# Two of seven weight rests made by a transfer that adds, in a two-block transformer kernel

## The chip, the cores and the metric

One core of one Trainium2 chip runs the whole kernel. The time is device time in microseconds of that core for one execution. Five engines have instruction streams of their own, and meet through semaphores: TensorE (PE; its weight loads are listed as PEld), VectorE (DVE), ScalarE (ACT), GpSimd (POOL) and SyncE (SP, here only a queue of transfers).

## The reference

The kernel computes a stack of transformer blocks on 512 tokens with a model width of 1024: a block with gated delta-rule attention and one with stick-breaking attention, each followed by a SwiGLU feed-forward layer, and then a third block with latent and windowed attention and a convolutional feed-forward layer. The change touches only the two SwiGLU layers:

```python
def swiglu(x, w_gu, w_down):
    g, u = jnp.split(x @ w_gu, 2, axis=-1)
    return (jax.nn.silu(g) * u) @ w_down

h = h + swiglu(rms_norm(h, ffn_norm[layer]), ffn_w_gu[layer], ffn_w_down[layer])
```

The gate and up matrices together are 1024 x 5632 and the down matrix 2816 x 1024, all float32. The result must hold to float32 accuracy.

## The kernel before, in words

**Products in three passes.** TensorE multiplies rounded float32 (the type fp32r). Every operand is therefore split into a rounded part (`wh`, `xh`) and its rest (`wl`, `xl`), and a product is three matmuls: rounded by rounded, rounded weight by rest of the input, rest of the weight by rounded input (`three`, lines 2331 to 2333). ScalarE makes the rounded part of a weight tile by a copy into fp32r, and VectorE the rest by a subtraction.

**The stream of weights.** All weights lie in one tensor, `stream`, as units of 128 x 2048 float32, 1 MB each. SP loads unit u into `raw[:, u % 2]` (`load`) once the unit that was there is used up: it waits for the semaphores `hi_made` and `lo_made`, which count units whose last quarter has been rounded and whose last rest is made.

**Seven products in place of eight.** The two SwiGLU layers ("ffn0" and "ffn1", function `ffn_fast` on each engine) hold most of their work as 24 units with a scheme of seven products of half size in place of eight (the Strassen-Winograd form). Tokens are halved (256 each), and a unit's four quarters of 128 x 512 are the four blocks of the weight matrix. Products 0, 1, 3, 5 and 6 read a quarter of `raw`, two of which VectorE has overwritten with sums by then; products 2 and 4 read the sums in `wsum`. A product is called a piece here: (j, k) is piece k of unit j. Of each unit, pieces 1 and 6 use quarters 1 and 3 as they came from memory. A piece is four blocks of three matmuls with 256 columns. The 24 units are 16 gate units (a gate tile and its up tile) and two groups of 4 down units.

**The order.** `ORDER` lists the 168 pieces of a layer: (0, 0), and then for each unit j the pieces 2, 1, 4, 3 of j, piece 0 of j + 1, and 5 and 6 of j. So piece (j, 6) stands at position 7j + 7. Each engine walks this list at its own step p, with fixed leads: at step p ScalarE copies out the result of the piece at p - 1 (pieces 0, 2, 4), does the silu if the piece at p - 2 was a 5, and rounds the weights of piece p + 5 (`HI_LEAD`); VectorE makes the rest of piece p + 4 (`LEAD`), the sums for piece p + 6 (`SUM_LEAD`), and joins or adds the result of piece p - 1; after a whole gate unit it multiplies gate and up (`gated`). In some units it also prepares a pair of hidden tiles as operands of the down products (`pair_sums`, `pair_lo`, lines 1397 to 1410; ScalarE does `pair_hi`). All of it is in order on each engine, so a wait holds everything behind it.

**Places of the pieces.** The rounded parts and rests have eight slots of 128 x 512 each; a slot is free when TensorE has done the piece eight positions before.

**The lines.** 657 is ScalarE's rounding of a piece (`hi`), 1483 VectorE's rest of a piece (`lo`), 1454 and 1456 the first two sums, 1461 and 1467 the other two, 617 the silu, 674 the copy out, 1498, 1504 and 1509 the joins of pieces 1, 3 and 5, 1520 the addition of a down piece, 1379 and 1380 the product of gate and up, 1366 the wide product of the six plain gate units that go before the stretch, 493 the load of the stream, 2253 GpSimd's eight transfers of 256 KB at another place of the kernel.

```python
def lo(j, k):
    half, w = weights_of(f, j, k)
    ...
    dve.tensor_tensor(wl[:, half, w], source_of(f, j, k), wh[:, half, w].bitcast(F32), ALU.subtract).then_inc(lo_made if k == 6 else part_lo, 1)
```

GpSimd does nothing in these stretches: it has a sum of squares before and one after.

Of the kernel before, what the change touches and what calls it, by code (L numbers as in the profile page):

```python
# [113 lines left out]
LEAD = 4  # L114
HI_LEAD = 5
SUM_LEAD = 6
SETS = ((4, 5, 0), (1, 2, 3))
BANK_OF = {0: 0, 2: 0, 3: 0, 6: 0, 1: 1, 4: 2, 5: 2}
QUARTER_OF = {0: (0, 0), 1: (0, 0), 2: (0, 1), 5: (0, 1), 4: (1, 1), 3: (1, 1), 6: (1, 0)}
# [39 lines left out]
SPLITS = running(lambda j, k: k != 6)  # L159
# [4 lines left out]
PAIR_SUMS_AT.update({DONE_AT[GATE_AT[2 * m + 1]] + 3: m for m in (3, 5, 6, 7)})  # L164
HIDDEN_AT = {DONE_AT[DOWN_AT[7]] + 1: REST, DONE_AT[DOWN_AT[7]] + 2: REST + 1}
HIDDEN_AT.update({DONE_AT[GATE_AT[n]] + 3: n for n in range(REST + 2, FC)})


def gu_count(f, n):
# [48 lines left out]
def build(nc, io):  # L218
    with ExitStack() as ctx:
# [137 lines left out]
        def mat(name):  # L357
# [60 lines left out]
        each = {part_hi: SPLITS[last_piece] + 3, part_lo: SPLITS[last_piece] + 3, prod_done: SPLITS[last_piece],  # L418
                weights_summed: 4 * len(STREAM), forked: FORKS[last_piece], joined: JOINS[last_piece], normed: 8,
                tokens_summed: 16, operand_hi: 12, operand_lo: 12, half_added: ADDS[last_piece], pair_summed: 4 * (REST // 2)}  # L420

        def fast_count(s, f, n):
            return before[s] + each[s] * f + n
# [15 lines left out]
        def piece_done(f, j, k):  # L439
            if k == 6:  # L440
                return units_used, stream_unit(FAST[f], j) + 1
            return prod_done, fast_count(prod_done, f, SPLITS[j, k])

        def slot_free(f, j, k):
            i = ORDER.index((j, k))
# [70 lines left out]
        def _(act):  # L516
# [92 lines left out]
            def ffn_fast(f, to, gain):  # L609
# [39 lines left out]
                def hi(j, k):  # L649
                    u = stream_unit(name, j)  # L650
                    half, w = weights_of(f, j, k)
                    if k in (2, 3, 4, 5):
                        act.wait_ge(weights_summed, fast_count(weights_summed, f, 4 * j + {4: 1, 2: 2, 3: 3, 5: 4}[k]))
                    else:
                        act.wait_ge(raw_landed[u % 2], 16 * (u // 2) + 16)
                    act.wait_ge(*slot_free(f, j, k))
                    act.activation(wh[:, half, w], source_of(f, j, k), ACT.Copy).then_inc(hi_made if k == 6 else part_hi, 1)  # L657

                def down_hi(q):
                    u = stream_unit(name, len(STREAM))  # L660
# [3 lines left out]
                    act.activation(wh[:, u % 2, w], raw[:, u % 2, w], ACT.Copy).then_inc(part_hi if q < 3 else hi_made, 1)  # L664

                def copy_out(j, k):
                    act.wait_ge(prod_done, fast_count(prod_done, f, SPLITS[j, k]))
                    last = gate_before(j)
                    if last is not None:
                        act.wait_ge(*join_made(f, last, {0: 1, 2: 5, 4: 3}[k]))  # L670
                    elif k == 4:
                        act.wait_ge(prod_made, FC * f + PLAIN)
                    to = scaled[:, 1, 0:TOK] if k == 4 else fork[:, k // 2, :]
                    act.activation(to, result_of(j, k), ACT.Copy).then_inc(forked, 1)

                def products():
                    for p in range(len(ORDER) + 4):
                        j, k = ORDER[p - 1] if 0 < p <= len(ORDER) else (None, None)
                        if j in GATES and k in (0, 2, 4):
                            copy_out(j, k)  # L680
                        j, k = ORDER[p - 2] if 1 < p <= len(ORDER) + 1 else (None, None)
                        if j in GATES and k == 5:
                            act.wait_ge(*join_made(f, j, 5))
                            silu(STREAM[j][1])
                        if p + HI_LEAD < len(ORDER):
                            hi(*ORDER[p + HI_LEAD])
                        elif p + HI_LEAD < len(ORDER) + 4:
# [11 lines left out]
                    token_sums(n)  # L699
                pair_hi(0)  # L700
                gate_up(4)
                for p in ORDER[:LEAD]:
                    hi(*p)
                gate_up(5)
                hi(*ORDER[LEAD])
                products()
                for i in range(3):
                    split_hi(u0 + 31 + i)
# [511 lines left out]
        def _(dve):  # L1220
# [50 lines left out]
            def split_out(name, to, gain):  # L1271

                u0, r = U0[name], RESID[name]
                for c in range(KC):
                    if c in (4, 6):
                        split_lo(u0 + 3 + (4, 6).index(c))
                    if c == KC - 1:
                        for x in range(KC - 1):
                            dve.wait_ge(resid_added, 8 * r + x + 1)
                            low_of_scaled(to, gain, x)  # L1280
                    if name == "mix_out":
                        dve.wait_ge(h_back[c], 16)
# [74 lines left out]
            def ffn_fast(f, to, to_gain):  # L1357
# [88 lines left out]
                def first_sums(j):  # L1446
                    u, q = stream_unit(name, j), raw_quarters(j)
                    dve.wait_ge(raw_landed[u % 2], 16 * (u // 2) + 16)
                    if j:
                        dve.wait_ge(part_lo, fast_count(part_lo, f, SPLITS[j - 1, 4]))  # L1450
# [12 lines left out]
                def last_sum(j):  # L1463
                    q = raw_quarters(j)
                    dve.wait_ge(weights_summed, fast_count(weights_summed, f, 4 * j + 2))
                    dve.wait_ge(part_lo, fast_count(part_lo, f, SPLITS[j, 1]))
                    dve.tensor_tensor(q[1], q[1], wsum[:, 1, :], ALU.subtract).then_inc(weights_summed, 1)

                def sums(j, k):
# [6 lines left out]

                def lo(j, k):
                    half, w = weights_of(f, j, k)
                    if k == 6:
                        dve.wait_ge(hi_made, stream_unit(name, j) + 1)  # L1480
                    else:
                        dve.wait_ge(part_hi, fast_count(part_hi, f, SPLITS[j, k]))
                    dve.tensor_tensor(wl[:, half, w], source_of(f, j, k), wh[:, half, w].bitcast(F32), ALU.subtract).then_inc(lo_made if k == 6 else part_lo, 1)  # L1483

                def down_lo(q):
                    u = stream_unit(name, len(STREAM))
                    w = slice(SEQ * q, SEQ * q + SEQ)
                    if q < 3:
                        dve.wait_ge(part_hi, fast_count(part_hi, f, SPLITS[last_piece] + q + 1))
# [31 lines left out]

                def products():
                    for p in range(len(ORDER) + 5):
                        if p + LEAD < len(ORDER):
                            lo(*ORDER[p + LEAD])
                        elif p < len(ORDER):
# [32 lines left out]
                pair_lo(0)  # L1559
                gate_up(4)  # L1560
                sums(*ORDER[1])
                for p in ORDER[:LEAD]:
                    lo(*p)
                sums(*ORDER[LEAD])
                gate_up(5)
                products()
# [595 lines left out]
        def _(pool):  # L2162
# [165 lines left out]
        def _(pe):  # L2328
# [115 lines left out]
            def ffn_fast(f):  # L2444
# [23 lines left out]
                def piece(j, k):  # L2468
                    kind, n = STREAM[j]
                    half, w = weights_of(f, j, k)  # L2470
                    if k == 6:
# [24 lines left out]
                def down_rest():  # L2496
                    u1, width = stream_unit(name, len(STREAM)), FC - REST
                    for i in range(3):
                        if i:
                            unit_ready(u1 + i)  # L2500
                        for b in (*range(5), *range(6, 11), 5, *range(11, BLOCKS)) if i == 0 else range(BLOCKS * i, BLOCKS * i + BLOCKS):
                            c, fc = b // width, b % width
                            if b in (0, 4, 8):
                                pe.wait_ge(part_hi, fast_count(part_hi, f, SPLITS[last_piece] + b // 4 + 1))
                                pe.wait_ge(part_lo, fast_count(part_lo, f, SPLITS[last_piece] + b // 4 + 1))
# [853 lines left out]
```

## Time and profile before

| | |
|---|---|
| Median of three runs | 2214.07 us (2213.58 to 2215.66) |
| The profiled execution | 2213.68 us, span 2211.8 us |
| Granted TensorE clock over the span | 0.997 |
| TensorE matmuls busy | 2147.3 us, 97% of the span |
| VectorE busy | 1460.8 us, 66% |
| ScalarE busy | 1082.7 us, 49% |
| GpSimd busy | 320.9 us, 15% |
| Transfers | 185.00 MB, mean 84 GB/s |

The busy time of an engine is the time in which it runs at least one instruction. TensorE's matmuls overlap and their ends are modelled, so the starts of successive matmuls say more than their lengths. A row of the timeline has the start from the beginning of the span, the duration, the engine, the line, the operation, its output and inputs with their shapes, and in brackets the idle time of the engine just before it, with the instruction that ended it.

### The profile page before, as it was taken

The page shows a single profiled execution, that of the slowest core. Times are in us where ns is not written, and L with a number is a line of the kernel's source. Part 1 is how long each engine was busy: PE and PEld are TensorE (multiplying, and loading weights), DVE is VectorE, ACT ScalarE, POOL GpSimd, SP SyncE. Part 2 cuts the span into 40 slices and gives each one's busy share as a digit, 9 for nine tenths or more (in the row PEclk, how much of TensorE's full clock was granted, in tenths as well). Part 3 has the DMA queues.
Part 4 walks back from the last instruction along what each step waited for, and adds up shares of the span by engine and source line. Part 5 has one row for each costly group of instructions (what it writes and reads, how often), then busy time and mean ns, then how long its engine had stood idle before and what let it go on. Part 6 is the DMA issues. An engine that isn't in the chain of part 4 may idle for free.

```text
span 2211.8 us, 33448 instructions
## 1 busy us (share of the span) xinstructions
PE 2147.3 (97%) x12698; PEld 1836.8 (83%) x12698; DVE 1460.8 (66%) x2344; ACT 1082.7 (49%) x1700; POOL 320.9 (15%) x267
## 2 busy tenths in 40 slices
PE   9999999998999999999999999999999999999998
PEld 6788887788999978877889989878778778888887
DVE  6766666479999843455689999556666665555522
ACT  5445555345454544565444555355565554444312
POOL 0221222310000030002200000300111144222211
PEclk9999999999999999999999999999999999999999
DMA  3311111221222322201213222331221222222221
GB/s 140 115 58 39 58 39 39 74 91 65 96 96 96 125 92 89 79 36 39 96 65 107 96 96 100 130 132 58 72 72 39 72 97 96 98 101 102 96 95 57
DMA packets 31675, 185.00 MB, mean 84 GB/s; under 512 B 3104, under 2 KB 7712, under 8 KB 11312
## 3 DMA queue, kind: packets, MB, share of 16 engines
q1 hardware_dynamic: 29520, 175.48, 22.9%
q0 software_dynamic: 2016, 7.60, 1.0%
q8 instruction: 95, 1.56, 0.3%
q14 instruction: 44, 0.36, 0.0%
HBM read 178.84 MB, written 7.37 MB: 84 GB/s over the span
## 4 chain that ended last, share of the span: by engine, by line
PE 74%; DVE 13%; ACT 5%; issue 4%; DMA 2%; SPq 0%; DVEq 0%; POOL 0%; ACTq 0%; POOLq 0%
PE ps L2331 20%; PE ps L2333 19%; PE ps L2332 19%; DVE wl L1483 3%; DMA raw<-in_stream 2%; PE ps L2657 2%; PE ps L3148 1%; ACT wh L525 1%; PE ps L3091 1%; PE ps L3131 1%; PE ps L2651 1%; DVE wsum L1454 1%; ACT wh L657 1%; PE ps L3158 1%; PE ps L2923 1%
## 5 line engine op out<-in xcount | busy, mean ns | idle before, releaser
L2331 PE MATMUL ps<-xh,wh 128*128 128x512 f32 (+1 forms) x1616 | 610.3, 378 | 13.3 <-DVE act_up L1380 9.4
L2333 PE MATMUL ps<-xh,wl 128*128 128x512 f32 (+1 forms) x1616 | 584.0, 361 | 0.0
L2332 PE MATMUL ps<-xl,wh 128*128 128x512 f32 (+1 forms) x1616 | 582.8, 361 | 0.0
L2331 PEld LDWEIGHTS ps<-xh,wh 128*128 128x128 f32 x1616 | 306.0, 189 | 63.4 <-issue 12.1
L2333 PEld LDWEIGHTS ps<-xh,wl 128*128 128x128 f32 x1616 | 305.1, 189 | 48.0
L2332 PEld LDWEIGHTS ps<-xl,wh 128*128 128x128 f32 x1616 | 306.0, 189 | 42.4 <-issue 4.3
L1229 DVE TENSOR_TENSOR wl<-raw,wh 128x2048 fp32r<-128x2048 f32 x92 | 212.8, 2313 | 175.7 <-ACT wh L525 175.6
L525 ACT ACTIVATE wh<-raw 128x2048 fp32r<-128x2048 f32 x92 | 175.9, 1912 | 161.1 <-PE ps L2333 160.8
L2331 PE MATMUL ps<-part_h,wh 128*128 128x256 f32 (+1 forms) x672 | 221.7, 330 | 6.0 <-DVE hT L1520 3.9
L2333 PE MATMUL ps<-part_h,wl 128*128 128x256 f32 (+1 forms) x672 | 220.3, 328 | 0.0
L2332 PE MATMUL ps<-part_l,wh 128*128 128x256 f32 (+1 forms) x672 | 219.8, 327 | 0.0
L657 ACT ACTIVATE wh<-raw 128x512 fp32r<-128x512 f32 x240 | 146.2, 624 | 96.6 <-DMA raw<-in_stream 57.6
L1483 DVE TENSOR_TENSOR wl<-raw,wh 128x512 fp32r<-128x512 f32 x240 | 165.1, 688 | 36.8 <-ACT wh L657 36.6
L2331 PE MATMUL ps<-t_h,wh 128*128 128x256 f32 x512 | 146.4, 286 | 17.7 <-DVE scaled L1504 10.7
L2331 PEld LDWEIGHTS ps<-part_h,wh 128*128 128x128 f32 x672 | 126.2, 188 | 22.0 <-issue 5.9
L2333 PE MATMUL ps<-t_h,wl 128*128 128x256 f32 x512 | 143.7, 281 | 0.0
L2332 PE MATMUL ps<-t_l,wh 128*128 128x256 f32 x512 | 143.6, 280 | 0.0
L2332 PEld LDWEIGHTS ps<-part_l,wh 128*128 128x128 f32 x672 | 126.0, 188 | 12.5 <-issue 0.5
L2333 PEld LDWEIGHTS ps<-part_h,wl 128*128 128x128 f32 x672 | 126.3, 188 | 11.3
L2331 PEld LDWEIGHTS ps<-t_h,wh 128*128 128x128 f32 x512 | 97.1, 190 | 21.8 <-issue 12.8
L2170 POOL TENSOR_TENSOR ssq<-hT 128x512 f32<-128x512 f32 x6 | 6.2, 1040 | 716.7 <-DVE hT L1579 659.9
L2333 PEld LDWEIGHTS ps<-t_h,wl 128*128 128x128 f32 x512 | 97.1, 190 | 0.0
(427 smaller groups left out, 4069.0 us busy)
## 6 DMA issues: line engine op xcount, KB each, us to landing
raw<-in_stream SPq DMA_DIRECT2D x158, 1024.0 KB, 4.8
hankd<-tabd SPq DMA_DIRECT2D x1, 3072.0 KB, 17.3
hank<-hankd POOLq DMA_DIRECT2D x4, 768.0 KB, 5.1
hT<-in_xT SPq DMA_DIRECT2D x4, 512.0 KB, 6.1
keepd<-hT POOLq DMA_DIRECT2D x1, 2048.0 KB, 10.1
hT<-keepd POOLq DMA_DIRECT2D x8, 256.0 KB, 4.8
out<-hT SPq DMA_DIRECT2D x8, 256.0 KB, 2.5
raw<-in_stream SPq DMA_DIRECT2D x2, 512.0 KB, 7.7
```

The lines of the kernel that those rows point to most:

```text
L525: act.activation(wh[:, s, :], raw[:, s, :], ACT.Copy).then_inc(hi_made, 1)
L657: act.activation(wh[:, half, w], source_of(f, j, k), ACT.Copy).then_inc(hi_made if k == 6 else part_hi, 1)
L1229: dve.tensor_tensor(wl[:, s, :], raw[:, s, :], wh[:, s, :].bitcast(F32), ALU.subtract).then_inc(lo_made, 1)
L1454: dve.tensor_tensor(wsum[:, 0, :], q[2], q[3], ALU.add).then_inc(weights_summed, 1)
L1483: dve.tensor_tensor(wl[:, half, w], source_of(f, j, k), wh[:, half, w].bitcast(F32), ALU.subtract).then_inc(lo_made if k == 6 else part_lo, 1)
L2331: pe.matmul(out, w_hi, a_hi, start=start, stop=False, skip_group_check=goes_on)
L2332: pe.matmul(out, w_hi, a_lo, start=False, stop=False, skip_group_check=goes_on)
L2333: return pe.matmul(out, w_lo, a_hi, start=False, stop=stop, skip_group_check=goes_on)
L2651: m = pe.matmul(ps[:, b, cs(c)], left[:, c, :], right[:, c, :], start=True, stop=True)
L2657: m = pe.matmul(part(ps[:, b, cs(c)]), left[:, c, :], part(right[:, c, :]), start=True, stop=True)
L2923: pe.matmul(part(z_tri, kb), kT[:, h, kb * P:(kb + 1) * P], q_sb[:, h % 2, kb * P:SEQ], start=True, stop=False)
L3091: pe.matmul(ps[:, bank, :], qn[:, c, q], kn[:, c, :], start=False, stop=True).then_inc(sc_done, 1)
```

## The change

For pieces 1 and 6 of every seven-product unit, VectorE's subtraction is left out. ScalarE writes the rounded part into `wh`, as before, and then a second time, negated, into `wl`. GpSimd waits for that and issues a transfer of the same quarter from the weight stream in memory, 128 x 512 float32 or 256 KB, which adds to what stands in `wl`. TensorE waits for the transfer's semaphore. There are 24 units x 2 pieces x 2 layers = 96 such transfers. ScalarE rounds these pieces six positions ahead in place of five (function `rounded_in`). The semaphores that release the next load of the stream, and with it `unit_ready`, now go with piece 5 in place of piece 6. The sum that overwrites quarter 1 waits for the rounding of piece 1, no longer for its rest. The counters are split accordingly (`HIGHS`, `RESTS`, `DONE`), and two semaphores of a later stage count the landings.

```diff
+ADDED_BY_DMA = (1, 6)
...
+def rounded_in(p):
+
+    if p == -2:
+        return ORDER[:LEAD]
+    at = [(p + SUM_LEAD, True), (p + HI_LEAD, False)]
+    return [ORDER[i] for i, by_dma in at if LEAD <= i < len(ORDER) and (ORDER[i][1] in ADDED_BY_DMA) == by_dma]
...
-                    act.activation(wh[:, half, w], source_of(f, j, k), ACT.Copy).then_inc(hi_made if k == 6 else part_hi, 1)
+                    if k in ADDED_BY_DMA:
+                        act.activation(wh[:, half, w], source_of(f, j, k), ACT.Copy)
+                        act.activation(wl[:, half, w], source_of(f, j, k), ACT.Copy, scale=-1.0).then_inc(part_hi, 1)
+                    else:
+                        act.activation(wh[:, half, w], source_of(f, j, k), ACT.Copy).then_inc(hi_made if k == 5 else part_hi, 1)
...
-                        if p + HI_LEAD < len(ORDER):
-                            hi(*ORDER[p + HI_LEAD])
+                        for q in rounded_in(p):
+                            hi(*q)
...
-                    dve.wait_ge(part_lo, fast_count(part_lo, f, SPLITS[j, 1]))
+                    dve.wait_ge(part_hi, fast_count(part_hi, f, HIGHS[j, 1]))
                     dve.tensor_tensor(q[1], q[1], wsum[:, 1, :], ALU.subtract).then_inc(weights_summed, 1)
...
-                        if p + LEAD < len(ORDER):
+                        if p + LEAD < len(ORDER) and ORDER[p + LEAD][1] not in ADDED_BY_DMA:
                             lo(*ORDER[p + LEAD])
...
+            def weight_rests(f):
+
+                for j, k in [q for q in ROUNDED if q[1] in ADDED_BY_DMA]:
+                    half, w = weights_of(f, j, k)
+                    q = {1: 1, 6: 3}[k]
+                    landed, n = rest_by_dma(f, j, k)
+                    pool.wait_ge(part_hi, fast_count(part_hi, f, HIGHS[j, k]))
+                    if n > 16:
+                        pool.wait_ge(landed, n - 16)
+                    pool.dma_start(wl[:, half, w], io["stream"][stream_unit(FAST[f], j)][:, SEQ * q:SEQ * q + SEQ], accum_op=ALU.add).then_inc(landed, 16)
...
             sum_squares("ffn0")
+            weight_rests(0)
...
             sum_squares("ffn1")
+            weight_rests(1)
...
-                    if k == 6:
+                    if k == 5:
                         unit_ready(stream_unit(name, j))
                     else:
-                        pe.wait_ge(part_hi, fast_count(part_hi, f, SPLITS[j, k]))
-                        pe.wait_ge(part_lo, fast_count(part_lo, f, SPLITS[j, k]))
+                        pe.wait_ge(part_hi, fast_count(part_hi, f, HIGHS[j, k]))
+                        pe.wait_ge(*(rest_by_dma(f, j, k) if k in ADDED_BY_DMA else (part_lo, fast_count(part_lo, f, RESTS[j, k]))))
```

## Rows read from the trace of the kernel before

**Rows 1.** Busy time by stretch: two layers' pieces, a start, one period.
```profile
core 0: us, PE busy (x) PEld busy (x) DVE busy (x) ACT busy (x) POOL busy (x), PEclk, DMA share, GB/s
511.41:772.54 261.13, 245.29 (x2017) 241.42 (x2016) 238.53 (x461) 135.91 (x267) 0.00 (x0) 0.99 0.28 98
1133.64:1393.98 260.34, 245.07 (x2018) 241.30 (x2016) 238.59 (x461) 136.10 (x267) 0.00 (x0) 0.99 0.28 98
516.00:522.00 6.00, 5.54 (x34) 5.57 (x35) 5.93 (x13) 4.07 (x10) 0.00 (x0) 0.72 0.01 3
657.43:680.26 22.83, 20.61 (x169) 20.02 (x169) 20.59 (x41) 12.66 (x27) 0.00 (x0) 1.00 0.25 94
```

**Rows 2.** Waits of TensorE, 511 to 773: total us, times, longest.
```profile
PE ps L2331 <- DVE scaled L1504: 5.6, 5, 1.4
PE ps L2331 <- DVE act_up L1380: 4.6, 5, 1.4
PE ps L2331 <- DVE hT L1520: 2.2, 4, 0.9
```

**Rows 3.** Timeline of TensorE, first matmuls of blocks.
```profile
511.41 0.28 PE L2331 MATMUL ps<-xh,wh 128*128 128x256 f32 x1
...
516.46 0.35 PE L2331 MATMUL ps<-t_h,wh 128*128 128x256 f32 x1 [3.46 <-DVE wl L1483]
...
657.43 0.35 PE L2331 MATMUL ps<-t_h,wh 128*128 128x256 f32 x1 [1.43 <-DVE scaled L1504]
...
765.78 0.28 PE L2331 MATMUL ps<-xh,wh 128*128 128x256 f32 x1
...
772.54 0.40 PE L2331 MATMUL ps<-part_h,wh 128*128 128x512 f32 x1
```

**Rows 4.** Timeline of VectorE in a gate unit.
```profile
661.14 0.41 DVE L1509 TENSOR_TENSOR scaled<-fork,ps 128x256 f32<-128x256 f32 x1
661.47 0.69 DVE L1483 TENSOR_TENSOR wl<-raw,wh 128x512 fp32r<-128x512 f32 x1
662.78 0.69 DVE L1483 TENSOR_TENSOR wl<-raw,wh 128x512 fp32r<-128x512 f32 x1 [0.62 <-ACT wh L657]
...
665.38 0.69 DVE L1483 TENSOR_TENSOR wl<-raw,wh 128x512 fp32r<-128x512 f32 x1
```

**Rows 5.** Timeline of ScalarE beside it, and its waits for the stream, 511 to 773.
```profile
661.59 0.64 ACT L617 ACTIVATE act_up<-scaled 128x512 f32<-128x512 f32 x1 [2.56 <-DVE scaled L1509]
662.13 0.62 ACT L657 ACTIVATE wh<-raw 128x512 fp32r<-128x512 f32 x1
...
671.18 0.63 ACT L657 ACTIVATE wh<-raw 128x512 fp32r<-128x512 f32 x1 [2.31 <-DMA raw<-in_stream]
...
ACT wh L657 <- DMA raw<-in_stream: 29.8, 17, 2.6
```

**Rows 6.** Timeline of SP's queue there: a load of the stream.
```profile
666.29 0.33 SPq L493 DMA_DIRECT2D raw<-in_stream  x1
```

**Rows 7.** GpSimd's 256 KB transfers (ns); their landing; the stream's, 511 to 773.
```profile
L2253 POOL DMA_DIRECT2D hT<-keepd x8: 537/539/590, 1812.8 to 1816.6; - x8
...
DMA to landing us min/median/max: 3.1/4.8/7.7
...
DMA to landing us min/median/max: 4.7/4.9/6.1
```

**Rows 8.** Timeline of VectorE and ScalarE at the start of the first stretch.
```profile
511.32 0.68 DVE L1483 TENSOR_TENSOR wl<-raw,wh 128x512 fp32r<-128x512 f32 x1
511.92 0.69 DVE L1483 TENSOR_TENSOR wl<-wsum,wh 128x512 fp32r<-128x512 f32 x1
...
513.12 1.22 DVE L1366 TENSOR_TENSOR scaled<-ps,rstd 128x1024 f32<-128x1024 f32 x1
...
511.11 0.62 ACT L657 ACTIVATE wh<-wsum 128x512 fp32r<-128x512 f32 x1
...
515.96 0.36 ACT L674 ACTIVATE fork<-ps 128x256 f32<-128x256 f32 x1
```

More of the change, by code:

```diff
@@ L158 @@
 DONE_AT = [ORDER.index((j, 6)) for j in range(len(STREAM))]
-SPLITS = running(lambda j, k: k != 6)
+DONE = running(lambda j, k: k != 6)
+RESTS = running(lambda j, k: k in (0, 2, 4, 3))
 FORKS = running(lambda j, k: STREAM[j][0] == "gate" and k in (0, 2, 4))
@@ L166 @@
 HIDDEN_AT.update({DONE_AT[GATE_AT[n]] + 3: n for n in range(REST + 2, FC)})
+def rounded_in(p):
[3 more added lines that the diff above has]
+    return [ORDER[i] for i, by_dma in at if LEAD <= i < len(ORDER) and (ORDER[i][1] in ADDED_BY_DMA) == by_dma]
+ROUNDED = [q for p in range(-2, len(ORDER)) for q in rounded_in(p)]
+HIGHS = {q: sum(k != 5 for _, k in ROUNDED[:i + 1]) for i, q in enumerate(ROUNDED)}
 def gu_count(f, n):
@@ L417, in build @@
         last_piece = ORDER[-1]
-        each = {part_hi: SPLITS[last_piece] + 3, part_lo: SPLITS[last_piece] + 3, prod_done: SPLITS[last_piece],
+        highs, rests = len(ORDER) - len(STREAM), RESTS[last_piece]
+        rest_added = {1: h_back[0], 6: h_back[1]}
+        each = {part_hi: highs + 3, part_lo: rests + 3, prod_done: DONE[last_piece],
                 weights_summed: 4 * len(STREAM), forked: FORKS[last_piece], joined: JOINS[last_piece], normed: 8,
@@ L441, in piece_done, with rest_by_dma @@
                 return units_used, stream_unit(FAST[f], j) + 1
-            return prod_done, fast_count(prod_done, f, SPLITS[j, k])
+            return prod_done, fast_count(prod_done, f, DONE[j, k])
+        def rest_by_dma(f, j, k):
+            return rest_added[k], 16 * (len(STREAM) * f + j + 1)
         def slot_free(f, j, k):
@@ L666, in copy_out @@
                 def copy_out(j, k):
-                    act.wait_ge(prod_done, fast_count(prod_done, f, SPLITS[j, k]))
+                    act.wait_ge(*piece_done(f, j, k))
                     last = gate_before(j)
@@ L684, in products @@
                             silu(STREAM[j][1])
-                        if p + HI_LEAD < len(ORDER):
-                            hi(*ORDER[p + HI_LEAD])
-                        elif p + HI_LEAD < len(ORDER) + 4:
+                        for q in rounded_in(p):
+                            hi(*q)
+                        if len(ORDER) <= p + HI_LEAD < len(ORDER) + 4:
                             down_hi(p + HI_LEAD - len(ORDER))
@@ L701, in ffn_fast @@
                 gate_up(4)
-                for p in ORDER[:LEAD]:
-                    hi(*p)
+                for q in rounded_in(-2):
+                    hi(*q)
                 gate_up(5)
-                hi(*ORDER[LEAD])
+                for q in rounded_in(-1):
+                    hi(*q)
                 products()
@@ L1281, in split_out @@
                     if name == "mix_out":
-                        dve.wait_ge(h_back[c], 16)
+                        dve.wait_ge(h_back[c], 16 * (2 * len(STREAM) if c < 2 else 0) + 16)
                     if c < 3:
@@ L1449, in first_sums @@
                     if j:
-                        dve.wait_ge(part_lo, fast_count(part_lo, f, SPLITS[j - 1, 4]))
+                        dve.wait_ge(part_lo, fast_count(part_lo, f, RESTS[j - 1, 4]))
                         dve.wait_ge(weights_summed, fast_count(weights_summed, f, 4 * j))
@@ L1478, in lo @@
                     half, w = weights_of(f, j, k)
-                    if k == 6:
+                    if k == 5:
                         dve.wait_ge(hi_made, stream_unit(name, j) + 1)
                     else:
-                        dve.wait_ge(part_hi, fast_count(part_hi, f, SPLITS[j, k]))
-                    dve.tensor_tensor(wl[:, half, w], source_of(f, j, k), wh[:, half, w].bitcast(F32), ALU.subtract).then_inc(lo_made if k == 6 else part_lo, 1)
+                        dve.wait_ge(part_hi, fast_count(part_hi, f, HIGHS[j, k]))
+                    dve.tensor_tensor(wl[:, half, w], source_of(f, j, k), wh[:, half, w].bitcast(F32), ALU.subtract).then_inc(lo_made if k == 5 else part_lo, 1)
                 def down_lo(q):
@@ L1488, in down_lo @@
                     if q < 3:
-                        dve.wait_ge(part_hi, fast_count(part_hi, f, SPLITS[last_piece] + q + 1))
+                        dve.wait_ge(part_hi, fast_count(part_hi, f, highs + q + 1))
                     else:
@@ L1523, in products @@
                     for p in range(len(ORDER) + 5):
-                        if p + LEAD < len(ORDER):
+                        if p + LEAD < len(ORDER) and ORDER[p + LEAD][1] not in ADDED_BY_DMA:
                             lo(*ORDER[p + LEAD])
-                        elif p < len(ORDER):
+                        elif len(ORDER) <= p + LEAD < len(ORDER) + 4:
                             down_lo(p + LEAD - len(ORDER))
@@ L1561, in ffn_fast @@
                 sums(*ORDER[1])
-                for p in ORDER[:LEAD]:
-                    lo(*p)
+                for j, k in ORDER[:LEAD]:
+                    if k not in ADDED_BY_DMA:
+                        lo(j, k)
                 sums(*ORDER[LEAD])
@@ L2470, in piece @@
                     half, w = weights_of(f, j, k)
-                    if k == 6:
+                    if k == 5:
                         unit_ready(stream_unit(name, j))
                     else:
-                        pe.wait_ge(part_hi, fast_count(part_hi, f, SPLITS[j, k]))
-                        pe.wait_ge(part_lo, fast_count(part_lo, f, SPLITS[j, k]))
+                        pe.wait_ge(part_hi, fast_count(part_hi, f, HIGHS[j, k]))
+                        pe.wait_ge(*(rest_by_dma(f, j, k) if k in ADDED_BY_DMA else (part_lo, fast_count(part_lo, f, RESTS[j, k]))))
                     if (j, k) == (0, 0):
@@ L2503, in down_rest @@
                             if b in (0, 4, 8):
-                                pe.wait_ge(part_hi, fast_count(part_hi, f, SPLITS[last_piece] + b // 4 + 1))
-                                pe.wait_ge(part_lo, fast_count(part_lo, f, SPLITS[last_piece] + b // 4 + 1))
+                                pe.wait_ge(part_hi, fast_count(part_hi, f, highs + b // 4 + 1))
+                                pe.wait_ge(part_lo, fast_count(part_lo, f, rests + b // 4 + 1))
                             if b == 11:
```

## The prediction

> **What bounds the kernel now.** I read the windows first. The two stretches in which all 336 pieces of the seven-product units run last 261.1 and 260.3 us [rows 1]. Then the matmul starts: a block of three matmuls of 256 columns follows the last after (772.54 - 765.78) / 19 = 0.356 us when nothing is late, so a piece of four blocks takes 1.42, a unit 9.96, and the 672 blocks of a stretch 239.1 us [rows 3]. TensorE loses 22.0 + 21.2 = 43.2 us in them, and that is all this change can reach; VectorE is busy for 238.5 of the 261.1 us, ScalarE for 136, GpSimd for none [rows 1]. The loss has three parts. (a) The second piece starts at 516.46, and the first, begun at 511.41, had ended at 512.83: 3.6 us in each stretch [rows 3]. (b) After that idle time the granted clock is 0.72 for 6 us, so 0.28 x 6 = 1.7 us in each, stayed at the lower of the two levels for a while. (c) What is left, 43.2 - 7.2 - 3.4 = 32.6 us, is steady. The waits of TensorE say whose it is: of 12.4 us of visible idle time in the first stretch 10.2 end with the sums of the gate units and 2.2 with those of the down units, all on VectorE [rows 2]. So 83% of (c), 27 us, belongs to gate units and 5.6 to down units.
>
> One period of two gate units shows the chain. From 657.43 to 680.26 are 22.83 us for 14 pieces that need 19.9: 2.9 lost. VectorE is busy for 20.59 of it and idle for 2.2 [rows 1, 3]: it is the bound, with gaps that ScalarE makes. Such a gap: the join of piece 5 starts at 661.14; ScalarE's silu starts at 661.59 behind it and the rounding of the next piece 5 at 662.13; the rest of that piece starts at 662.78, after 0.62 us idle [rows 4, 5]. In the next unit ScalarE had first waited 2.31 us for the stream's landing [rows 5].
>
> **The change, part by part.**
> Removed: of the seven subtractions of a unit on VectorE two go, 96 in all. They follow one another every 511.92 - 511.32 = 0.60 us [rows 8], so 1.2 us a unit, 58 us in all, beside TensorE but on the bound of (c).
>
> Added on ScalarE: 96 negated roundings. Its operations start 662.13 - 661.59 = 0.54 us apart [rows 5]: 1.08 us a unit, 52 us in all. ScalarE has room for the sum, but not everywhere for the place: pieces 1 and 6 are now rounded six ahead, the others five ahead, so both roundings of piece 6 stand between the silu and the rounding of piece 5. At the gap above the rest of piece 5 would start 1.08 us later, at 663.86, and VectorE would be idle for 1.7 us in place of 0.62. It hits every gate unit in which the join is already late.
>
> Period of two gate units after: busy 20.59 - 4 x 0.60 = 18.2, two gaps of 1.7 = 3.4, together 21.6 us against 22.83 now and 19.9 of TensorE.
>
> Moved: the next transfer of the stream waits for the rest of piece 5, no longer of piece 6. That rest now ends at 663.86 + 0.69 = 664.55, where piece 6 ended at 665.38 + 0.69 = 666.07, and the queue issued at 666.29 [rows 4, 6]: 1.5 us earlier. Against it stands traffic. A 256 KB transfer by GpSimd landed in 3.1 us at the least, the stream's 1024 KB in 4.9: 768 KB more in 1.8, so 0.6 us for each 256 KB [rows 7]. Two additions a unit share the engines with it; each moves 256 KB, or the worth of 512 if the read of its destination counts as much. That is 1.2 to 2.4 us, if all of it meets the stream's transfer. The two about cancel, and ScalarE's wait for the landing, which delays the silu by about 1 us in one unit of two (it holds ScalarE until 671.18), may stay. So the period is between 21.6 and 22.6; I take the middle, 22.1, since neither side is nearer a row. That gains 0.7 of 2.9, 24% of 27 = 6.5 us. In the down units there is no silu in the chain, and VectorE's 1.2 us come free: I take the whole 5.6 us.
>
> Start: VectorE skips the rest of piece 1 there, but ScalarE's extra rounding moves that of the fourth piece from 511.11 to 511.63, and it ends at 512.25. VectorE then does that rest and a sum of 0.60 each, and the wide product starts at 513.5, not at 513.12: the copy of 515.96, for which the second piece waits, and with it TensorE, come 0.4 us later, 0.8 in both stretches [rows 8]. Clock as in (b).
>
> The additions: GpSimd issues them in 0.54 us each, and had nothing else to do in the stretches [rows 1, 7]; what is queued behind its waits is the sum of squares of the next stage, which needs results from after the stretch. TensorE now waits for a landing in place of a subtraction. Call L the time from the negated rounding to the landing seen by TensorE. The room: a join ends about 0.5 us into piece 7j, the second rounding of piece 6 of that unit ends 0.04 + 0.54 + 0.54 + 0.62 = 1.74 later, and the piece's turn is at 9.96: 7.6 us are free for L (for piece 1, rounded two pieces later and used two later, about as much). Where a pair of hidden tiles is prepared VectorE falls behind: that is five narrow operations 0.33 us apart [rows 4] and three of 0.60, 3.5 us; without it a gate unit takes VectorE (18.2 - 3.5) / 2 + 1.7 = 9.05 us of 9.96. So it ends 3.5 - 0.9 = 2.6 us late, and 5.0 are left for L. The trace shows no accumulating transfer. Bounds by the nearest rows: 3.1 (a lone 256 KB) and 7.7 (the last of eight queued) [rows 7], plus 0.6 if the destination's read counts: 3.1 to 8.3. I take 4.5: the lone one, 0.6 for the read and 0.8 for the stream's transfer beside it, as only two are ever queued. Then it is hidden at no cost. If the cover goes, each microsecond of L over 7.6 costs one per gate unit.
>
> The Trainium skill ("Collectives: The Full Stack", Part 3, the bandwidth ceiling) says that an add in the transfer needs two source reads and so halves the rate of the same ring. "DMA: Bandwidth & Descriptors" (Anatomy of one DMA) fits 2.0 us plus bytes at 436 GB/s for GpSimd's transfers, an estimate of 2.6 us for 256 KB, where the row has 3.1 at the least; with the first rule it would be 3.2, and the sum would not move. No row here shows an add.
>
> Sum: 6.5 + 5.6 - 0.8 = 11.3 us. The profiled execution took 2213.7 us (span 2211.8), so 2202.4; the median of the runs stands 0.4 above it, so 2203.
>
> **Rivals.**
> 1. Everything steady goes. For: VectorE's load falls to 18.2 of 19.9 us in the worst period, so only gaps keep it behind, and where pairs are apart the lag may be absorbed. Against: the longer hand-off. 32.6 - 0.8 = 32 us faster: 2182.
> 2. The hand-off and the later landing take back what the subtractions gave: period 22.6 or more, the down units still held by the landing: 0.2 / 2.9 x 27 = 2 us or nothing, less 0.8. 2210 to 2216, no change that can be told (this kernel's runs can tell about 0.2%, 4.4 us). For it: ScalarE already waited 29.8 us for landings in the first stretch [rows 5].
> 3. The additions land late, slower. The loop is piece 7j done, join, silu, two roundings, transfer, piece 7j + 7: it decides from L = 7.6. Then the 14 pairs cost 2.6 us each, 36, in place of the 32.6 of now, already even; at 8.3, the upper bound, 0.7 x 32 gate units = 22 more: 2213.7 + 36 - 32.6 + 22 = 2239. At L = 10 the last term is 2.4 x 32 = 77, near 2294. For: two queues meet in bursts, and the landing of the stream reached 6.1 us alone [rows 7]; the add is unseen. Against: 7.6 us is more than twice what a lone 256 KB took.
>
> **How the numbers follow.** Forecast (2192 to 2209) 0.45; rival 1 0.12; rival 2 0.17; rival 3 0.26. Faster by over 0.2%: the forecast nearly whole and rival 1, 0.56; within: 0.16; slower: 0.28, rival 3 and a tail of rival 2. The range: 2188, short of rival 1, to 2232, into rival 3. The forecast's own range is 2192 to 2209: 2198 is the period of 21.6, the rest of each side is the clock and the down units.
>
> **What would show it.** 240 subtractions at the rest's line in place of 336, and 96 more roundings; TensorE's waits in the stretches still on VectorE's joins, shorter, none on GpSimd's transfers; landing of these near 4 to 5 us; VectorE's gaps before the rest of piece 5 near 1.7 us; the second piece near 516.9; the stretches 255 to 256 us. It is wrong if TensorE waits for landings, if these take over 7 us, or if the stream's own landing grows by over 1.5 us.

## The result, and the profile after

The changed kernel takes 2257.4 us (median of four runs, 2252.9 to 2262.7) against 2214.9, a ratio of 1.019 (95% interval 1.017 to 1.022): 42 us slower, where 11 us faster had been forecast. The profiled execution has a span of 2256.6 us, 44.8 more than before.

All of it lies in the two stretches. The windows of the changed kernel, each from the first matmul of the stretch, in the columns of [rows 1]:

```profile
512.14:793.18 281.04, 252.94 (x2018) 246.22 (x2016) 212.19 (x413) 158.83 (x315) 40.90 (x48) 0.98 0.55 136
1154.25:1439.50 285.25, 251.75 (x2018) 243.91 (x2016) 212.13 (x413) 159.06 (x315) 41.27 (x48) 0.99 0.55 134
```

They grew by 19.9 and 24.9 us, which is the 44.8. VectorE is relieved as planned (238.5 us of 261 before, 212.2 of 281 now) and ScalarE busy 23 us longer, but the transfer engines go from a share of 0.28 to 0.55. Their time in the first stretch rose from 0.28 x 261 = 73 us to 0.55 x 281 = 155, to 2.1 times, though the bytes rose only by half (98 GB/s over 261 us are 25.6 MB, 136 over 281 are 38.2). The page's queues, with packets, megabytes and share of the engines over the span, first of the changed kernel:

```profile
q1 hardware_dynamic: 29520, 175.48, 22.8%
q0 software_dynamic: 15840, 32.78, 7.9%
```

The queue of GpSimd had 1.0% for 7.6 MB before. So the 96 additions took 6.9% of 2256.6 us, 155.7 us of all engines: 1.62 us each. The stream takes 22.8% for 175.48 MB, 0.77 us for the same 256 KB.

The landings, first the stream's in the first stretch (4.7/4.9/6.1 in [rows 7]), then the additions' over the kernel, and one addition of a piece 1 with the matmul that needs it, the latter from TensorE's timeline:

```profile
DMA to landing us min/median/max: 4.8/7.6/10.5
...
DMA to landing us min/median/max: 4.2/5.1/10.1
...
672.04 0.85 POOL L2255 DMA_DIRECT2D wl<-in_stream  x1 [0.99 <-ACT wl L678]
...
680.50 0.36 PE L2369 MATMUL ps<-xh,wh 128*128 128x256 f32 x1 [1.26 <-DMA wl<-in_stream]
```

The stream is late. The 5.1 of the additions mixes two kinds, told apart by the piece that each belongs to. The 48 of pieces 6, mostly issued 1.2 us ahead of the load, landed in 4.4 us in the median and 5.5 at most, as forecast. The 48 of pieces 1 landed in 8.2 in the median, and 32 of them in more than 7.6. Mostly they are issued 0.4 to 0.7 us behind the load: the one above leaves at 672.04, the load at 671.38, and it landed after 8.3 us. TensorE's waits in the first stretch, beside [rows 2], and ScalarE's for the stream, beside [rows 5]:

```profile
PE ps L2369 <- DMA wl<-in_stream: 11.0, 11, 3.0
PE ps L2369 <- DVE hT L1544: 6.3, 8, 1.4
PE ps L2369 <- DVE wl L1507: 3.8, 1, 3.8
PE ps L2369 <- DVE act_up L1404: 3.5, 5, 0.8
PE ps L2369 <- ACT fork L697: 2.6, 4, 1.4
...
ACT wh L680 <- DMA raw<-in_stream: 51.7, 19, 6.0
```

TensorE now waits for additions too: 22.9 us in 25 waits over both stretches, each before a piece 1. That looks like the third rival; the experiments say otherwise. The timeline shows what goes round. One turn in the changed kernel, by engine (SP, GpSimd, ScalarE, VectorE):

```profile
671.38 0.33 SPq L512 DMA_DIRECT2D raw<-in_stream  x1
...
681.59 0.84 POOL L2255 DMA_DIRECT2D wl<-in_stream  x1 [8.69 <-ACT wl L678]
682.76 0.33 SPq L512 DMA_DIRECT2D raw<-in_stream  x1
...
679.10 0.63 ACT L680 ACTIVATE wh<-raw 128x512 fp32r<-128x512 f32 x1 [3.19 <-DMA raw<-in_stream]
679.64 0.61 ACT L636 ACTIVATE act_up<-scaled 128x512 f32<-128x512 f32 x1
680.16 0.61 ACT L677 ACTIVATE wh<-raw 128x512 fp32r<-128x512 f32 x1
680.68 0.61 ACT L678 ACTIVATE wl<-raw 128x512 fp32r<-128x512 f32 x1
681.20 0.61 ACT L680 ACTIVATE wh<-raw 128x512 fp32r<-128x512 f32 x1
...
681.85 0.69 DVE L1507 TENSOR_TENSOR wl<-raw,wh 128x512 fp32r<-128x512 f32 x1 [1.39 <-ACT wh L680]
```

A load is issued at 671.38 and lets ScalarE go on at 679.10. ScalarE works in order: piece 0 of the new unit, then the silu, both roundings of piece 6, then piece 5; VectorE makes the rest of 5, and only that releases the next load, at 682.76. The turn takes 11.4 us, and TensorE needs 9.96 for a unit. The addition of piece 6 goes out at 681.59, 1.2 us before the load.

Not every turn is like this one. Where ScalarE waits for the stream and no pair is prepared, the next load follows the landing after 3.68 us in gate units and 3.16 in down units (5.24 and 4.79 in the kernel before), so there the turn is the landing plus a constant. A turn in which VectorE prepares a pair lasts 13.15 us in the changed kernel and as long without the transfers, whatever the landing.

A part of the loss is clock. The granted clock, before and in two places of the changed kernel:

```profile
516.00:524.00 8.00, 7.54 (x51) 7.57 (x52) 7.93 (x17) 5.68 (x13) 0.00 (x0) 0.79 0.15 35
```
```profile
516.00:524.00 8.00, 6.48 (x33) 6.51 (x34) 6.81 (x14) 6.48 (x15) 0.85 (x1) 0.57 0.46 87
772.00:780.00 8.00, 6.64 (x34) 6.67 (x35) 4.86 (x10) 6.06 (x12) 1.70 (x2) 0.57 0.32 63
```

At the start of each stretch (0.79 - 0.57) x 8 = 1.8 us more were lost than before, and 3.4 us near 775: some 7 of the 44.8.

### The profile page after: what moved, and what is told of

Its sections match the earlier page's. It is cut to its first block, busy times and chain, and to the rows that moved or that the text cites. A ratio compares the mean times of both kernels' runs of the same rounds, so it can differ in the third digit from the quotient of the medians.

```text
span 2256.6 us, 33638 instructions
## 1 busy us (share of the span) xinstructions
PE 2161.6 (96%) x12698; PEld 1844.3 (82%) x12698; DVE 1408.6 (62%) x2248; ACT 1127.0 (50%) x1796; POOL 403.0 (18%) x363
## 3 DMA queue, kind: packets, MB, share of 16 engines
q1 hardware_dynamic: 29520, 175.48, 22.8%
## 4 chain that ended last, share of the span: by engine, by line
PE 68%; DVE 9%; DMA 8%; ACT 7%; issue 7%; SPq 0%; POOL 0%; DVEq 0%; ACTq 0%; POOLq 0%
PE ps L2369 18%; PE ps L2371 17%; PE ps L2370 17%; DMA raw<-in_stream 6%; DMA wl<-in_stream 2%; PE ps L2695 2%; PE ps L3186 1%; ACT wh L544 1%; PE ps L3129 1%; PE ps L3169 1%; PE ps L2689 1%; DVE wl L1507 1%; ACT wh L677 1%; ACT wh L680 1%; PE ps L3196 1%
## 5 line engine op out<-in xcount | busy, mean ns | idle before, releaser
L2255 POOL DMA_DIRECT2D wl<-in_stream x96 | 82.2, 856 | 588.0 <-ACT wl L678 571.5
L1507 DVE TENSOR_TENSOR wl<-raw,wh 128x512 fp32r<-128x512 f32 x144 | 99.0, 689 | 120.2 <-ACT wh L680 120.2
L680 ACT ACTIVATE wh<-raw 128x512 fp32r<-128x512 f32 x144 | 89.4, 623 | 137.7 <-DMA raw<-in_stream 112.5
L2370 PEld LDWEIGHTS ps<-t_l,wh 128*128 128x128 f32 x512 | 98.3, 192 | 0.0
```

Of the source, the lines that this page charges most:

```text
L2255: pool.dma_start(wl[:, half, w], io["stream"][stream_unit(FAST[f], j)][:, SEQ * q:SEQ * q + SEQ], accum_op=ALU.add).then_inc(landed, 16)
L2370: pe.matmul(out, w_hi, a_lo, start=False, stop=False, skip_group_check=goes_on)
```

## The experiments

The theories: A, the loop of the stream's load, lengthened by the traffic; B, the longer hand-off on ScalarE alone; C, TensorE's direct waits for the additions. All ratios are to the kernel before on the same chip.

**Without the transfers.**

```diff
-            weight_rests(0)
...
-                        pe.wait_ge(*(rest_by_dma(f, j, k) if k in ADDED_BY_DMA else (part_lo, fast_count(part_lo, f, RESTS[j, k]))))
+                        if k not in ADDED_BY_DMA:
+                            pe.wait_ge(part_lo, fast_count(part_lo, f, RESTS[j, k]))
```

> The changed kernel with both ScalarE roundings, but without the 96 transfers and without TensorE's wait for them (the third product of pieces 1 and 6 then uses the negated rounded part). Theory A, the stream's loop under more traffic (landing of a stream unit 7.6 us in place of 4.9, and the loop landing, ScalarE in order, rest of piece 5, next load is longer than TensorE's 9.96 us): landing back at 4.9, loop about 4.9 + 3.9 = 8.8, time 2190 to 2205. Theory B, the hand-off on ScalarE (two roundings between silu and piece 5): stays at 2240 to 2257. Theory C, TensorE's waits for the additions themselves (22.9 us in the profile): about 2257 - 23 - 5 for the clock = 2229.

2205.3 us, ratio 0.995 (0.994 to 0.997). The stream lands in 4.8 us, and ScalarE waits for it 4.3 us in all of the first stretch, where it had waited 51.7. B falls as the main cause: with both roundings in place the kernel is faster than before. The transfers cost 2257.4 - 2205.3 = 52 us.

**The additions, but TensorE does not wait.**

```diff
-m = three(result_of(j, k), wh[:, half, blk], wl[:, half, blk], ...)
+m = three(result_of(j, k), wh[:, half, blk], (wh if k in (1, 6) else wl)[:, half, blk], ...)
...
+                    if landed_before(f, j, k):
+                        dve.wait_ge(*landed_before(f, j, k))
```

> The changed kernel with all 96 adding transfers, but TensorE does not wait for them: the third product of pieces 1 and 6 reads the rounded part instead of the rest, and only the next writer of the place waits for the landing, eight pieces later. Theory A: the stream's landing stays above 7 us, only the 22.9 us of direct waits can go, and some of them turn into waits for the stream: 2235 to 2252. Theory B: the same 2235 to 2252. Theory C: 2190 to 2205, as without transfers.

2259.2 us, ratio 1.021 (1.018 to 1.023): nothing gained, less even than A had allowed. The stream lands in 7.7 us, and ScalarE waits for it 59.9 us in the first stretch. C falls: the 22.9 us of direct waits come back as waits for other things, since something else sets the pace.

**The kernel before, with the additions beside it.**

```diff
+            def added(f):
+                for j, k in [q for q in ORDER if q[1] in (1, 6)]:
+                    ...
+                    pool.dma_start(wl[:, half, w], io["stream"][...], accum_op=ALU.add).then_inc(landed, 16)
```

> The kernel before, VectorE making every rest as ever, plus the 96 adding transfers into the same places once the rest is made; TensorE reads the rounded part in place of the rest for pieces 1 and 6 and does not wait for a transfer. Only traffic is added. Theory A: the stream lands in 7 us or more, and the loop of the kernel before (4.9 + 5.0 us now) becomes 12 or more: 2240 to 2300. Theories B and C: 2213 to 2217, as before.

2241.6 us, ratio 1.012 (1.010 to 1.014): the traffic alone costs 27 us, with VectorE doing all its work. The size of A's landing was missed: the stream landed in 5.7 us, not 7. Here the load was issued just ahead of the addition of piece 6 (660.71 and 660.79 us in its timeline), and the addition landed late instead, in 7.0 us. The places' next writers also wait for the landing, so a part of the 27 us may be theirs.

**Piece 5 rounded before piece 6.**

```diff
-    at = [(p + SUM_LEAD, True), (p + HI_LEAD, False)]
+    at = [(p + HI_LEAD, False), (p + SUM_LEAD, True)]
```

> The changed kernel with ScalarE rounding piece 5 before both roundings of piece 6 (same six and five ahead); the next load waits for the negated rounding of 6 and the rest of 5, which now run beside each other. VectorE's gap before the rest of piece 5 falls by 1.04 us, the load goes out about 0.7 us earlier, the addition of piece 6 0.52 later. Theory A: 0.7 us of the loop in up to 48 units, less the later addition: 2225 to 2245. Theory B: the hand-off is as before the change: 2200 to 2215. Theory C: the addition lands 0.5 us later, 2257 to 2275.

2223.5 us, ratio 1.004 (1.002 to 1.005), 34 us less than the changed kernel, from the order of three instructions, and just under A's range. The landing of the stream fell from 7.6 to 5.5 us; the load now mostly leaves first:

```profile
665.47 0.33 SPq L512 DMA_DIRECT2D raw<-in_stream  x1
665.60 0.84 POOL L2255 DMA_DIRECT2D wl<-in_stream  x1 [9.17 <-ACT wl L678]
...
672.43 0.35 PE L2369 MATMUL ps<-t_h,wh 128*128 128x256 f32 x1 [2.01 <-issue]
```

What is left sits at piece 6: its addition was issued at 665.60, TensorE came to it with nothing to do and started at 672.43, 6.8 us later. The row names no releaser, but the addition's landing does: it came at 672.34, 0.09 us before. Nine such gaps, of 0.6 to 2.1 us, lie in the first stretch, each about 0.09 us behind the landing of the addition of a piece 6, mostly where VectorE had a pair to prepare. That is the mechanism of rival 3, in a kernel whose loop is shorter. The gaps also cost clock: the granted clock was 0.96 and 0.97 in the two stretches, about 10 and 7 us of their time, where the kernel before lost 1.7 in each.

**The addition of piece 6 after the load.**

```diff
+                    if k == 6:
+                        pool.wait_ge(lo_made, stream_unit(FAST[f], j) + 1)
```

> The changed kernel, only that GpSimd issues the addition of piece 6 after the rest of piece 5 is made, so about when the next stream load goes out and no longer 1.2 us before it. Nothing else moves. Theory A1 (the addition ahead of the load takes the transfer engines first, and the load lands late, which goes round the loop): landing of the stream back near 5.5 us, the additions about 1 us later; 2215 to 2238. Theory A2 (the traffic as such, whatever the order): landing stays near 7.6, additions later: 2257 to 2275.

2239.6 us, ratio 1.011 (1.009 to 1.013), 18 us less by one more wait, 2 us short of the range. The stream lands in 5.7 us instead of 7.6, with the same transfers: the order of issue sets the landing. The additions land in 6.8 instead of 5.1 (those of piece 6 in 6.8 instead of 4.4), and TensorE waits for those of piece 6 up to 2.3 us in the first stretch, so a part of the gain is given back.

**Plain transfers.**

```diff
-... SEQ * q:SEQ * q + SEQ], accum_op=ALU.add).then_inc(landed, 16)
+... SEQ * q:SEQ * q + SEQ]).then_inc(landed, 16)
```

> The changed kernel with plain transfers of the same 256 KB in place of the adding ones (the rest of pieces 1 and 6 is then the whole weight). If the read of the destination and the add make the cost (engine time of an adding transfer about twice a plain one's): landing of the stream 6 to 6.5 us, of the transfers near 4, 2220 to 2240. If the bytes from memory and the place in the queue alone count: landing and time as the changed kernel, 2250 to 2260.

2208.3 us, ratio 0.997 (0.996 to 0.998), better than expected. Of the 52 us of the transfers 49 belong to the addition: the bytes from memory and the order of issue are the same. The landing of its stream, of its transfers, and its queue on the page:

```profile
DMA to landing us min/median/max: 4.7/5.3/6.8
DMA to landing us min/median/max: 3.2/3.9/7.5
...
q0 software_dynamic: 15840, 32.78, 5.4%
```

A plain transfer of GpSimd took (5.4 - 1.0)% of 2208 / 96 = 1.01 us of the engines, an adding one 1.62, in as many packets.

**Piece 6 seven ahead.** Both of its roundings then stand before the silu.

```diff
+    at = [(p + 7, (6,)), (p + SUM_LEAD, (1,)), (p + HI_LEAD, (0, 2, 3, 4, 5))]
```

> The changed kernel with both roundings of piece 6 seven positions ahead in place of six, so before the silu; piece 1 stays at six. The hand-off silu, piece 5 is as before the change, and the addition of 6 is issued about 1.5 us earlier against its turn. If the loop and the late additions of piece 6 are the cost: 2195 to 2215. If the addition ahead of the load (A1) is all that counts, it still holds the load up: 2225 to 2250.

2207.6 us, ratio 0.997 (0.996 to 0.998), 50 us less than the changed kernel. The landings of the stream and of the additions in the first stretch, and the chain on ScalarE and VectorE:

```profile
DMA to landing us min/median/max: 4.7/6.5/8.4
DMA to landing us min/median/max: 4.2/4.7/9.6
...
680.23 0.63 ACT L636 ACTIVATE act_up<-scaled 128x512 f32<-128x512 f32 x1 [1.57 <-DVE scaled L1533]
680.77 0.61 ACT L680 ACTIVATE wh<-raw 128x512 fp32r<-128x512 f32 x1
...
681.42 0.69 DVE L1507 TENSOR_TENSOR wl<-raw,wh 128x512 fp32r<-128x512 f32 x1 [0.62 <-ACT wh L680]
```

The stream still lands in 6.5 us, and that costs little now: ScalarE waits for it 5.4 us in the first stretch, where it had waited 51.7. With the two roundings out, the way from a landing to the next load is 0.54 + 0.54 + 0.62 + 0.69 and 0.2 for the issue, 2.6 us; with 6.5 that is 9.1, under 9.96. Single landings still pass it: those of 7.4 to 8.4 us, where the addition went out 2.1 to 2.6 us before the load; where it was 3.9 us, the load landed in 5.3 to 5.6. So neither the landing nor the roundings alone make the loss: their sum passed the turn of TensorE. It also takes the gap before the rest of piece 5 back to 0.62 us in the row above.

**And piece 0 after piece 5.**

```diff
+    at = [(p + 7, (6,)), (p + SUM_LEAD, (1,)), (p + HI_LEAD, (2, 3, 4, 5)), (p + LEAD, (0,))]
...
+def rests_in(p):
+    at = [(p + LEAD, (2, 3, 4, 5)), (p + LEAD - 1, (0,))]
```

> As the one with piece 6 seven ahead, and besides the rounding and the rest of piece 0, which are the first to need a newly landed unit, come after those of piece 5 on ScalarE and VectorE. A late landing then no longer holds the silu, the rest of piece 5 and the next load: the loop is cut. Theory A: at or below the kernel before, 2183 to 2205. If the additions are late for TensorE by themselves: about as the one with piece 6 seven ahead.

2199.2 us, ratio 0.993 (0.992 to 0.995): faster than the kernel before and than the last version. In the first stretch its additions still land in 5.1 and its stream in 6.7 us, but no wait of TensorE or ScalarE ends with a transfer (in the second TensorE waits 2.3 us for additions, in three waits); TensorE's are these:

```profile
PE ps L2376 <- ACT fork L704: 5.6, 5, 4.3
PE ps L2376 <- DVE act_up L1411: 4.1, 5, 0.9
```

**That order in the kernel before.**

```diff
+    at = [(p + lead, (1, 2, 3, 4, 5, 6)), (p + lead - 1, (0,))]
```

> The kernel before, VectorE making all rests, only with the rounding and the rest of piece 0 after those of piece 5, as in the last run. If the late landing held the kernel before too (ScalarE waited 57.6 us for landings) and VectorE's load does not matter: 2203 to 2209. If VectorE's load is its bound (92% busy in the stretches), cutting the loop gives it nothing: 2212 to 2216. The rest of piece 6 still releases the load there.

2215.7 us, ratio 1.000 (0.999 to 1.001). The order gives nothing while VectorE makes all the rests, though the loop there, 4.9 + 5.2 = 10.1 us in gate units without a pair, was just over TensorE's 9.96. The gain needs VectorE's relief.

**The last but one without the transfers.**

```diff
-            weight_rests(0)
-            weight_rests(1)
```

> The fastest order so far (piece 6 seven ahead, piece 0 last) without the 96 transfers and TensorE's wait for them; the third product of pieces 1 and 6 uses the negated rounded part. If the additions are now hidden: within 3 us of 2199. If their traffic or latency still costs: 2188 to 2194.

2199.0 us, ratio 0.993 (0.991 to 0.994): 0.2 us from the kernel with them. In the right order the 96 additions are hidden, to within about 3 us: this run's profile was longer at the lower clock at the start of each stretch (granted 0.57 over 516 to 524 us, 0.79 with the additions), which is 1.8 us a stretch.

**Both pieces seven ahead.**

```diff
+    at = [(p + 7, (1, 6)), (p + HI_LEAD, (2, 3, 4, 5)), (p + LEAD, (0,))]
```

> As piece 6 seven ahead and piece 0 last, with piece 1 seven ahead too. Its addition is issued one piece earlier. TensorE waited in all 1.1 us for transfers in the second stretch there, so at most 1 to 2 us: 2196 to 2201. If the two additions then meet the load more: up to 2206.

2202.2 us, ratio 0.994 (0.993 to 0.995): above the 2196 to 2201 expected, and by the intervals not to be told from the 2199.2 with only piece 6 seven ahead and piece 0 last. The waits that it was to remove were 2.3 us, not 1.1; it has 3.1 us of such waits in its first stretch, one of 2.0.

## Why the prediction was wrong

The starts of successive silus give the periods, worked out from ScalarE's timeline. Three kinds from the first stretch, in us: two gate units of which one prepares a pair; the turn without the pair in it; and the five units across the second group of down units.

| kernel | pair of gate units | the shorter of the two | across the down group |
|---|---|---|---|
| before | 22.7 to 23.2 | 10.0 to 10.5 | 49.6 |
| changed | 22.9 to 24.7 | 9.8 to 11.5 | 55.1 |
| no transfers | 22.4 to 22.6 | 9.3 to 9.5 | 50.2 |
| 6 seven ahead | 20.9 to 22.2 | 8.8 to 10.1 | 51.6 |
| 6 seven ahead, 0 last | 21.6 to 22.1 | 8.9 to 9.4 | 49.7 |

**The failed step** is "The two about cancel, and ScalarE's wait for the landing, which delays the silu by about 1 us in one unit of two (it holds ScalarE until 671.18), may stay." Two things in it were wrong. The load was issued 1.6 us earlier behind the silu, as forecast (679.64 to 682.76, where it had been 661.59 to 666.29), but after the addition of piece 6, and landed 2.7 us later than before (7.6 against 4.9), where at most 2.4 was taken. And the two were set against each other as shifts of the kernel before, and the wait priced as a delay of a silu that is there anyway. They are parts of one loop, and the loop was never added up and held against TensorE's 9.96: 7.7 + 3.7 = 11.4 us, the two extra roundings (1.08 us) among the 3.7. Without the load's delay it would have been 4.9 + 3.7 = 8.6. What it cost is 52 us, by the run without transfers; 49 of them vanish with a plain transfer, and 50 with the roundings of piece 6 before the silu.

**The bound.** Right for the kernel before: VectorE with gaps of ScalarE in the gate units (the share of the gate units is 10.2 of 12.4, 82%, not 83). The unchanged 2215.7 us of the reordered kernel before bears it out.

**The relief of VectorE and the hand-off.** Without the transfers the time was 9.1 us less than before, where 11.3 was the sum: near, but partly by luck. The period of two gate units was to be 21.6 to 22.6 and came to 22.5 there, near its worse end. The parts missed: the down units were to give 5.6 us over both layers. By the silus the four groups lasted 201.4 us before and 201.7 without transfers, so they gave nothing; 20 units of 9.96 are 199.2, and only 2.2 were to be had. Of the 8.2 us by which the two profiles differ, 5.4 came from the first gate units of each layer, up to the first group of down units, for which one period from the middle had been taken.

**The down units under the transfers.** They had been taken as safe, with no silu in the chain. But the loop is there too: with the stream landing in about 7.8 us it is 7.8 + 3.16 = 11.0. The four groups took 227.3 us in the changed kernel, 25.9 more, over half of the 44.8.

**The start.** Forecast 0.4 us late in each stretch; the gap before the second piece went from 3.46 to 3.78, 0.3. "Clock as in (b)" did not hold in the changed kernel's profile, which lost 1.8 us more at each start; without the transfers the clock was as before.

**The additions.** One L was taken for both pieces, 4.5. It was right for piece 6 (landing 4.4 in the median) and wrong for piece 1 (8.2, and over the 7.6 of rival 3 in 32 of 48), which goes out just behind the load and lands about when the load does; 0.8 us had been taken for the load beside it. Two of the prediction's signs of being wrong came by this: TensorE waited for landings, and many took over 7 us. Yet the run in which TensorE did not wait gained nothing. So rival 3 came true in sign and in its late landings, but in the changed kernel its limit is not what decides. It does show where the loop is shorter, in the run with piece 5 first.

**Rivals 1 and 2.** Rival 1, 2182, was reached by no run; the best was 2199.0. The hand-off left the kernel without transfers faster than before, so rival 2 fails; it was not free, as without transfers the last order (2199.0) is 6.3 us under the first (2205.3). VectorE's gap did become 1.39 to 1.66 us, where 1.7 was said.

The Trainium skill ("Collectives: The Full Stack", Part 3, the bandwidth ceiling) says of a collective's add that it reads two sources and so halves the rate. Here an adding transfer took 1.62 us of the engines against 1.01 plain, so 1.6 times and not twice; the measurement decides. By the Trainium skill ("DMA: Bandwidth & Descriptors", Anatomy of one DMA) 256 KB take 2.6 us, an estimate. The plain ones here landed in 3.2 at the least, 0.6 above it; 0.53 of the 3.2 is the issue instruction.

What stays open: why an addition issued 1.2 us ahead makes the load land 2.7 us later where it occupies the engines for 1.6; and how the 27 us of the additions beside the kernel before divide between the load and the waits for the places.

## What to carry to other kernels

When a step is moved onto the transfer engines, price it where it meets the load that feeds the pipeline, and follow the load's loop once round: landing, every in-order instruction until the buffer is free, issue. If that sum passes the turn of the bound engine, the excess is paid in each turn that nothing longer sets, and a microsecond anywhere in the loop is worth as much as one of landing. Before giving up such a change, try the order: here two instructions moved ahead of a wait turned 42 us of loss into a gain of 7, and 16 us were gained in all against the kernel before with the first user of new data put last. And split a median by what each transfer stands behind: the 5.1 us of the additions was 4.4 for one piece and 8.2 for the other.

## What the runs showed of the hardware

An adding transfer of 256 KB is dearer on each count than a plain one from the same queue: GpSimd's issue took 0.85 us against 0.53, the landing 4.2 us against 3.2 at the least (5.1 and 3.9 in the median), the engines 1.62 against 1.01. The issue instructions, durations in ns, first of the changed kernel, then of the one with plain transfers:

```profile
L2255 POOL DMA_DIRECT2D wl<-in_stream x96: 844/854/1034, 512.7 to 1429.3; - x96
```
```profile
L2255 POOL DMA_DIRECT2D wl<-in_stream x96: 531/531/702, 512.2 to 1381.9; - x96
```

The landing of a 1 MB load went by when the nearest addition of piece 6 was issued, over both stretches of each trace:

| addition, against the load | the load landed in | kernels |
|---|---|---|
| none | 4.9 us (median) | before |
| 3.8 to 3.9 us ahead | 5.0 to 5.6 (23 loads) | the three with piece 6 seven ahead |
| 2.1 to 2.6 us ahead | 6.6 to 8.5 | the same three |
| 1.2 us ahead | 6.1 to 10.5, about 7.7 in the median | changed |
| 0.1 to 0.3 us behind | 5.2 to 6.0 (four of 121: 6.8 to 7.3) | before with the additions, piece 5 first, addition after the load |
| plain transfer, 1.2 us ahead | 4.9 to 7.6, 5.3 in the median | plain transfers |

A long wait also costs clock. TensorE of the changed kernel idled 3.0 us, and its blocks then followed at 0.64 us in place of 0.356, with a granted clock of 0.57 over 772 to 780 us:

```profile
773.36 0.55 PE L2369 MATMUL ps<-xh,wh 128*128 128x256 f32 x1 [2.99 <-DMA wl<-in_stream]
774.13 0.41 PE L2369 MATMUL ps<-xh,wh 128*128 128x256 f32 x1
774.77 0.41 PE L2369 MATMUL ps<-xh,wh 128*128 128x256 f32 x1
775.41 0.41 PE L2369 MATMUL ps<-xh,wh 128*128 128x256 f32 x1
```

That is how it went at the start of each stretch before [rows 1, 3]. After the waits of up to 1.6 us of the kernel before the blocks came at 0.356 again at once. In the version with piece 5 first they came at 0.64 after all seven waits of 1.8 to 2.2 us, as after the one at 672.43, but not after one of 2.9 us in the second stretch, so the length of the one wait does not settle it.
